# Where a forget bias is added: matrix products against a table, or rows sent through DRAM and added on VectorE

## The chip, the cores and the metric

One core of a Trainium2 chip runs the whole program. The core has TensorE (PE, matrix products and transposes; its weight loads are shown as PEld), VectorE (DVE), ScalarE (ACT), GpSimd (POOL), and SyncE (SP), which issues most of the DMAs. The metric is the device time of one launch in microseconds, lower is better. All data are float32.

## The reference, cut to what matters

The program is one inference step of a hybrid decoder layer for a prompt of 256 tokens and for 8 samples of 8 new tokens each. After one input projection there are a recurrent branch and an attention branch with 16 heads of 64; their merge goes through an output projection, and a mixture of experts (32 experts, 4 of them for each token) follows. The part that the change touches is the attention of the samples, whose keys and values come from 2 cached pages of 128 rows and from the 8 new tokens:

```
lf_all = concat([cache_logf[page_table].reshape(db, past, N_HEADS), logf], axis=1)   # past = 256
ft = swapaxes(cumsum(lf_all, axis=1), 1, 2)
sc = einsum('bqhd,bkhd->bhqk', q, k_all) * scale
bias = ft[:, :, past:, None] - ft[:, :, None, :]
p = softmax(where(mask, sc + bias, -inf), axis=-1)
```

The term of the query is the same for all keys of a row, and a softmax doesn't see it. Both kernels leave it out and add only minus the running sum: one row of 264 numbers for each sample and head, 128 rows in all.

## The kernel before, in words

The instruction streams are written out by hand, one for each engine. Each engine runs its own list in order, and semaphores join them. The pools of memory are few: `ring` (12 units of 2 x 128 x 2048) holds weights, cached keys and values, and, in units 4 and 5 (`fr`), small tables; PSUM has 8 banks, `B[0]` to `B[7]`.

The stages are: conditioning and input projection (to about 195 us), attention of the prompt beside the gate projections (`gate_job`, to about 284 us), attention of the samples beside the last gate jobs and the output projection (to about 378 us), norms and routing (to about 414 us), and then the experts, which read 400 MB of weights through the ring.

What counts here:

- **The cached log-forget pages.** SP loads 16 pages (8 samples, 2 pages, each 128 rows x 16 heads) into `lfc`. In head pair 6 of the prompt's attention, TensorE runs `cached_logf`: 16 products of a 32-column block against the identity, and 4 more for the new tokens, which lay the rows of sample b in the partitions 32 (b mod 4) to 32 (b mod 4) + 15, with the samples 4 to 7 beside the samples 0 to 3. Half of the partitions stay unused.
- **The running sums.** After the last head pair, VectorE copies these rows to `Fs` (L1168 to L1173), scans them in two halves (L1175) and changes the sign (L1176). The semaphore `F_made` reaches 2.
- **The scores of a sample.** `sscores(b)` makes 8 products of queries and keys into `B[2]` (L1733; each is recorded as two instructions, as all float32 products are), and then adds the bias by two more products, of the selection table `hsel` with the rows in `Fs`: 256 columns for the past (L1735), 8 columns for the new tokens (L1736). In `B[2]` the 128 partitions are the 16 heads by the 8 queries.
- **The softmax of a sample.** On VectorE `sample_max(b)` copies the 256 columns from PSUM to `Ss` (L1116), adds the mask to the other 64 (L1117) and takes the maximum (L1120). ScalarE takes the exponential, `sample_norm(b)` scales on VectorE (L1124, L1125), and TensorE turns the result (`sweights`), multiplies it with the values (`svalues`) and folds the heads (`sfold`).
- **The order on TensorE around it.** Gate job `gb` 2, `values(7)`, `sscores(0)`, gate job `gb` 3, `sscores(1)`, `sweights(0)`, and then for b = 0 to 7: a gate job (b < 4) or a quarter of the output projection, `svalues(b)`, `sscores(b+2)`, `sfold(b)`, `sweights(b+1)`. `sscores(b)` waits until `sample_max(b-1)` has read `B[2]` (semaphore `sscores_read`).
- **The order on SP around it.** `values_in(1)`, `chunk(23)`, `chunk(25)` (half of `w_out`, issued when gate job `ga` 7 is done), `keys_in(2)` (8 DMAs of 128 KB), `keys_in(3)`, `chunk(24)`, `keys_in(4)`, and then values and keys in turn. The keys go to two buffers and are turned by VectorE (`keys_turned`, L1108).
- **The join with the experts.** SP issues the first weights of the experts as the last samples free ring units; the ring holds a bit less than one pair of experts, and SP then waits until TensorE has used a unit.

## Time and profile before

| | us |
|---|---|
| median of 3 runs | 1372.84 (1371.81 to 1375.29) |
| the profiled execution, its own time | 1371.63 |
| its span, first to last instruction | 1369.9 |
| TensorE busy | 1302.4 (95%) |
| VectorE busy | 356.7 (26%) |
| ScalarE busy | 207.6 (15%) |
| mean granted TensorE clock | 0.989 |

TensorE is busy nearly throughout, but in the stage of the experts its busy time covers short waits for weights: matrix products are pipelined, and a product that waits inside counts as busy. The chain of waits names both, TensorE and the DMAs of the experts' weights. VectorE, ScalarE and GpSimd have idle time in every stage, which costs nothing unless TensorE or SP waits for them.

### The profile page before, as it was taken

How to read it: one execution, taken by the hardware profiler on the slowest of the kernel's cores; microseconds unless marked ns; L12 is line 12 of the kernel's file. 1: busy time of each engine (PE TensorE's matmuls, PEld its weight loads, DVE VectorE, ACT ScalarE, POOL GpSimd, SP SyncE). 2: the span in 40 equal slices, each digit the busy share in tenths (PEclk: the TensorE clock that was granted, in tenths of full speed). 3: DMA queues.
4: the chain of work that ended last, by engine and by line, in shares of the span. 5: the costliest groups of instructions: out<-in, count | busy, mean ns of one | idle time of the engine just before them, and what ended most of it. 6: DMA issues, size and time to landing. Idle time of an engine off the chain costs nothing.

```text
span 1369.9 us, 15525 instructions
## 1 busy us (share of the span) xinstructions
PE 1302.4 (95%) x6186; PEld 578.7 (42%) x6186; DVE 356.7 (26%) x754; ACT 207.6 (15%) x475; POOL 38.4 (3%) x79
## 2 busy tenths in 40 slices
PE   5999999999999999999999999999999999999896
PEld 3556466655463433434334343333434343343332
DVE  2541325756462121112112111221211121121112
ACT  1124424412221110101001010110101011010101
POOL 1100002000020000000000000000000000000000
PEclk9999999999999999999999999999999999999998
DMA  9836476779676999999999999999999999999992
GB/s 343 281 136 278 185 268 178 217 226 263 222 292 250 416 429 428 427 427 426 427 427 428 428 428 428 427 428 422 428 424 428 428 425 428 422 428 427 428 428 109
DMA packets 71904, 491.06 MB, mean 358 GB/s; under 512 B 11813, under 2 KB 24861, under 8 KB 44052
## 3 DMA queue, kind: packets, MB, share of 16 engines
q1 hardware_dynamic: 68564, 480.86, 86.8%
q0 software_dynamic: 3264, 9.13, 2.5%
q8 instruction: 55, 0.90, 0.3%
q14 instruction: 21, 0.17, 0.0%
HBM read 484.77 MB, written 5.18 MB: 358 GB/s over the span
## 4 chain that ended last, share of the span: by engine, by line
PE 58%; DMA 36%; DVE 2%; issue 1%; SPq 1%; ACT 0%; DVEq 0%; ACTq 0%
DMA ring<-in_w_gate_up_dram 34%; PE bank L1944 23%; PE bank L1627 8%; PE bank L1653 4%; PE bank L1932 2%; PE bank L2002 2%; PE bank L1615 2%; PE bank L1782 2%; PE bank L1567 2%; PE bank L1501 2%; PE bank L2030 1%; PE bank L1935 1%; PE bank L1908 1%; PE bank L1757 1%; DMA ring<-in_cache_k_dram 1%
## 5 line engine op out<-in xcount | busy, mean ns | idle before, releaser
L1944 PE MATMUL bank<-ring,work 128*64 128x512 f32 x1984 | 441.9, 599 | 15.3 <-DMA ring<-in_w_gate_up_dram 9.4
L1944 PEld LDWEIGHTS bank<-ring,work 128*64 128x64 f32 x1984 | 156.4, 138 | 286.7 <-issue 286.7
L1944 PE MATMUL bank<-ring,hT 128*64 128x512 f32 x896 | 201.3, 596 | 11.8 <-DMA ring<-in_w_gate_up_dram 11.6
L1444 DVE TENSOR_TENSOR gbT<-gbT,bank 128x512 f32<-128x512 f32 x80 | 55.0, 688 | 439.2 <-PE bank L1935 304.1
L1944 PEld LDWEIGHTS bank<-ring,hT 128*64 128x64 f32 x896 | 67.8, 137 | 142.5 <-issue 142.5
L1627 PE MATMUL bank<-hT,ring 128*128 128x320 f32 x384 | 106.3, 436 | 1.6 <-DVE hT L910 1.6
L1400 DVE TENSOR_SCALAR work<-bank 128x512 f32<-128x512 f32 x32 | 22.0, 686 | 315.9 <-PE bank L1944 295.4
L1627 PEld LDWEIGHTS bank<-hT,ring 128*128 128x128 f32 x384 | 71.8, 190 | 36.8 <-issue 4.0
L1653 PE MATMUL bank<-hT,ring 128*128 128x320 f32 x256 | 73.6, 437 | 0.2 <-ACT gaT L700 0.2
L1932 PE MATMUL bank<-work 128*128 128x512 f32 x128 | 67.8, 631 | 0.0
L837 ACT ACTIVATE work<-bank 128x320 f32<-128x320 f32 x15 | 6.6, 437 | 395.9 <-PE bank L1501 395.9
L1908 PE MATMUL bank<-qT,tok 128*128 128x256 f32 x224 | 63.3, 405 | 0.0
L1653 PEld LDWEIGHTS bank<-hT,ring 128*128 128x128 f32 x256 | 46.9, 190 | 19.7 <-issue 2.0
L1501 PE MATMUL bank<-ident,work 128*128 128x128 f32 (+4 forms) x250 | 44.5, 297 | 8.8 <-DMA work<-in_b_ada_dram 4.0
L1908 PEld LDWEIGHTS bank<-qT,tok 128*128 128x128 f32 x224 | 37.9, 189 | 28.2 <-issue 25.3
L850 ACT ACTIVATE work<-bank 128x512 f32<-128x512 f32 x30 | 16.3, 594 | 205.7 <-PE bank L1944 205.7
L1501 PEld LDWEIGHTS bank<-ident,work 128*128 128x128 f32 (+4 forms) x250 | 30.6, 175 | 34.8 <-issue 26.2
L840 ACT ACTIVATE work<-work 128x512 f32<-128x512 f32 x30 | 18.9, 630 | 144.6 <-DVE work L1400 144.6
L1932 PEld LDWEIGHTS bank<-work 128*128 128x128 f32 x128 | 20.4, 188 | 46.6 <-issue 46.6
L1909 PE MATMUL bank<-qT,tok 64*128 64x256 f32 x112 | 39.0, 428 | 0.0
L1567 PE MATMUL bank<-ring 128*32 128x512 f32 x192 | 26.3, 675 | 10.2 <-DMA ring<-in_w_ada_dram 10.2
L2002 PE MATMUL bank<-ring,hT 128*64 128x512 f32 x128 | 29.0, 597 | 0.0
(375 smaller groups left out, 911.4 us busy)
## 6 DMA issues: line engine op xcount, KB each, us to landing
ring<-in_w_gate_up_dram SPq DMA_DIRECT2D x128, 2048.0 KB, 16.2
ring<-in_w_down_dram SPq DMA_DIRECT2D x64, 2048.0 KB, 17.3
ring<-in_w_ada_dram SPq DMA_DIRECT2D x12, 2048.0 KB, 10.7
ring<-in_w_in_dram SPq DMA_DIRECT2D x12, 2048.0 KB, 10.8
ring<-in_cache_k_dram SPq DMA_DIRECT2D x64, 128.0 KB, 5.9
ring<-in_cache_v_dram SPq DMA_DIRECT2D x16, 512.0 KB, 5.7
ring<-in_w_out_dram SPq DMA_DIRECT2D x2, 2048.0 KB, 12.2
out_dram<-tok POOLq DMA_DIRECT2D x2, 1024.0 KB, 8.1
```

Of the source, the lines that this page charges most:

```text
L1444: TTo(piece(gbf, i), piece(gbf, i), B[6 + n % 2][:, :], ALU.add).then_inc(s["scatter_read"], 1)
L1501: return nc.tensor.transpose(out, in_, ident[0:rows, 0:rows])
L1567: last = mm(B[3][32 * g:32 * g + 32, :], silu_c[:, 2 * n + k, :], w_[:, k, 512 * g:512 * g + 512], start=(part == 0 and n == 0 and k == 0) ...
L1615: last = mm(ps[:, :], hT[:, k, 128 * n:128 * n + 128], w[0][:, k, :], start=(k == 0), stop=(k == NT - 1))
L1627: last = mm(ps[:, 0:T], w[0][:, k, 128 * (t % 4):128 * (t % 4) + 128], hT[:, k, :], start=(k == 0), stop=(k == NT - 1))
L1653: last = mm(gate_bank(i)[:, 0:T], wg[kind][:, k, 128 * (t % 4):128 * (t % 4) + 128], hT[:, k, :], start=(k == 0), stop=(k == NT - 1))
L1782: last = mm(B[5 + h][:, :], gaT[:, k, 128 * t:128 * t + 128], wo[h][:, k, :], start=(k == 0), stop=(k == NT - 1))
L1908: mm(out, tok[:, k, 128 * m:128 * m + 128], sel[:, k, :], start=(k == 0), stop=False)
L1909: last = mm(out, tok[q:q + 64, 2, 128 * (m % 4):128 * (m % 4) + 128], sel[q:q + 64, 2, :], start=False, stop=True)
L1932: last = mm(bank[:, :], C[:, 128 * k:128 * k + 128], Ysb[:, 512 * (i % 2):512 * (i % 2) + 512], start=True, stop=True)
L1944: last = mm(bank[CAP * x:CAP * x + CAP, :], lhsT[:, CAP * x:CAP * x + CAP], rhs(x), start=start, stop=stop)
L2002: last = mm(B[x + 2 * q][CAP * h:CAP * h + CAP, :], slots[:, k, CAP * x:CAP * x + CAP], gu_slot[4 * x + k // 2][:, k % 2, 1024 * q + 512 * ...
```

## The change

- The pages are laid out in `lfc` so that one 128-column block holds page i of all 8 samples. `cached_logf` becomes two 128x128 transposes and one small product for the new tokens (`lfnew` by `at_token`). Every partition then holds one sample and head: partition 16 b + h.
- The new tokens' values are spread into `lfnew` by one VectorE instruction; two small tables (`in_sample`, `at_token`) are made at the start. The table `hsel` and its four copies go.
- The sign is changed by the copy out of PSUM, and one scan does all rows. This work moves on VectorE ahead of `keys_turned(0)` and the last outputs of the prompt.
- SP writes the 128 rows to DRAM (`sample_bias`, `sample_tail`: 16 DMAs of 16 rows each), waits until they have landed, and reads them back so that each row lies in the 8 partitions of its head's queries: 8 DMAs of 128 KB to the place of the prompt's queries in `qT`, and one of 32 KB (`Ftail`).
- `sscores` loses its two bias products. `sample_max` adds the bias with the copy out of PSUM (`tensor_tensor` instead of `tensor_copy`), and adds the tail to the 8 new columns with one more instruction. `sample_max(0)` waits for the DMAs.

```diff
@@ sync
             chunk(25)
             keys_in(2)
+            eng.wait_ge(s["F_made"], 2)
+            for b in range(DB):
+                rows = Fs[H * b:H * b + H, :]
+                eng.dma_start(sbias_d[b].rearrange("u g n -> g u n"), rows[:, 0:PAST]).then_inc(s["bias_out"], 16)
+                eng.dma_start(stail_d[:, :, b, :].rearrange("u g q -> g u q"), rows[:, PAST:PAST + DS]).then_inc(s["bias_out"], 16)
+            eng.wait_ge(s["bias_out"], 16 + 32 * DB)
+            eng.wait_ge(s["scores_ps"], H)
+            for b in range(DB):
+                eng.dma_start(qT[:, b, 0:PAST], sbias_d[b].rearrange("u g n -> (u g) n").unsqueeze(1).to_broadcast([H, DS, PAST])).then_inc(s["bias_in"], 16)
+            eng.dma_start(Ftail, stail_d.rearrange("u g b q -> (u g) (b q)").unsqueeze(1).to_broadcast([H, DS, NS])).then_inc(s["bias_in"], 16)
             keys_in(3)
             chunk(24)
@@ vector, sample_max
-                V_.tensor_copy(P[:, 0:PAST], ps[:, 0:PAST]).then_inc(s["sscores_read"], 1)
+                if b == 0:
+                    eng.wait_ge(s["bias_in"], 96 + 16 + 16 * DB)
+                TTo(P[:, 0:PAST], ps[:, 0:PAST], qT[:, b, 0:PAST], ALU.add).then_inc(s["sscores_read"], 1)
...
+                new = P[:, PAST + DS * b:PAST + DS * b + DS]
+                link(TTo(new, new, Ftail[:, DS * b:DS * b + DS], ALU.add))
@@ tensor, cached_logf
+                eng.wait_ge(s["sample_consts"], 1)
+                for i in range(NPG):
+                    tr(B[1][:, 128 * i:128 * i + 128], lfc[:, DB * i:DB * i + DB, :].rearrange("p b h -> p (b h)"), 128)
+                mm(B[0][:, 0:DS], lfnew, at_token, start=True, stop=True).then_inc(s["tr_ps"], 1)
@@ tensor, sscores
-                        mm(ps[32 * g:32 * g + 32, 0:PAST + NS], Qbd[:, b % 2, t, :], KT[:, b % 2, t, :],
-                           start=(odd == 0), stop=False)
-                mm(ps[:, 0:PAST], hsel[q:q + H, :], Fs[q:q + H, n, 0:PAST], start=False, stop=False)
-                mm(ps[:, PAST + DS * b:PAST + DS * b + DS], hsel[q:q + H, :], Fs[q:q + H, n, PAST:PAST + DS], start=False, stop=True)\
-                    .then_inc(s["sscores_ps"], 1)
```

SP between `keys_in(2)` and `keys_in(3)` before: the last of the 8 DMAs of one is followed by the first of the next (TENSOR_LOAD and ISA read the page's number).

```order
L431 DMA ring<-in_cache_k_dram 32x4x256
L336 TENSOR_LOAD tiny [waits KT_made]
L336 ISA x2
L431 ISA
L431 DMA ring<-in_cache_k_dram 32x4x256
```

And with the change, the start and the end of what stands there now:

```order
L433 DMA ring<-in_cache_k_dram 32x4x256
L457 DMA sample_bias<-ring 4x4x256 [waits F_made]
L458 DMA sample_tail<-ring 4x4x8
...
L462 DMA qT<-sample_bias 128x1x256 [waits scores_ps,bias_out]
L462 DMA qT<-sample_bias 128x1x256 x7
L463 DMA ring<-sample_tail 128x1x64
L338 TENSOR_LOAD tiny [waits KT_made]
```

25 DMAs and two waits stand between the two loads of keys; `keys_in(3)` and all that SP issues after it come behind them.

VectorE before, from the last output of the prompt to the maximum of sample 0 (L1086 is `head_out`, L1187 makes `fold8`):

```order
L1187 TENSOR_REDUCE work<-ident 128x32 [waits chain_dve]
L1102 COPY work<-qT 32x8x8 x4
L1086 COPY gbT<-bank 128x256 [waits py_ps]
L1116 COPY work<-bank 128x256 [waits sscores_ps]
L1117 TENSOR_TENSOR work<-bank,ring 128x64
L1120 TENSOR_REDUCE tiny<-work 128x1 [waits sscores_read]
```

And with the change, to the turning of the keys of sample 2 (L1159 and L1160 are `gate_tile`, L1141 and L1142 `sample_norm`, L1121 `keys_turned`):

```order
L1199 TENSOR_REDUCE work<-ident 128x32 [waits chain_dve]
L1115 COPY work<-qT 32x8x8 x4
L1099 COPY gbT<-bank 128x256 [waits py_ps]
L1131 TENSOR_TENSOR work<-bank,qT 128x256 [waits bias_in,sscores_ps]
L1132 TENSOR_TENSOR work<-bank,ring 128x64
L1136 TENSOR_TENSOR work<-work,ring 128x8 [waits sscores_read]
L1137 TENSOR_REDUCE tiny<-work 128x1 [waits chain_dve]
L1159 SCALAR_TENSOR_TENSOR gbT<-ring,gbT 128x256 [waits py_read,job_ev]
L1160 SCALAR_TENSOR_TENSOR gaT<-gaT,gbT 128x256 [waits chain_dve]
L1141 RECIPROCAL tiny<-tiny 128x1 [waits sexp_done]
L1142 TENSOR_SCALAR work<-work,tiny 128x320 [waits chain_dve]
L1121 STREAM_TRANSPOSE work<-ring 128x8x8x32 [waits sscores_ps,k_in0]
```

The wait on `bias_in` is new and stands ahead of everything that VectorE does for the samples; the addition of 8 columns is new in each sample.

## Rows read from the trace of the kernel before

**Rows 1.** The page: the chain that ended last, shares by engine.

```profile
PE 58%; DMA 36%; DVE 2%; issue 1%; SPq 1%; ACT 0%; DVEq 0%; ACTq 0%
```

**Rows 2.** Stretches: us, busy us of each engine (instructions), TensorE clock, DMA share, GB/s.

```profile
310.00:320.00 10.00, 10.00 (x85) 6.21 (x84) 6.82 (x18) 1.80 (x6) 0.00 (x0) 1.00 1.11 267
...
410.00:420.00 10.00, 7.71 (x41) 3.02 (x39) 6.98 (x19) 3.35 (x5) 0.00 (x0) 1.00 0.01 2
```

**Rows 3.** TensorE in order of time (start, us, what, [idle before]), `cached_logf`.

```profile
269.49 1.06 PE L1700 MATMUL bank<-ident,ring 128*32 128x128 f32 x8
...
274.36 2.42 PE L1653 MATMUL bank<-hT,ring 128*128 128x320 f32 x8
```

**Rows 4.** The same view, TensorE around the first samples.

```profile
290.22 1.28 PE L1733 MATMUL bank<-work 128*32 128x320 f32 x16 [1.63 <-DVE work L1102]
...
296.69 1.28 PE L1733 MATMUL bank<-work 128*32 128x320 f32 x16
297.90 0.69 PE L1735 MATMUL bank<-ring,vecT 16*128 16x256 f32 x2
298.44 0.28 PE L1736 MATMUL bank<-ring,vecT 16*128 16x8 f32 x2
298.65 0.55 PE L1501 MATMUL bank<-ident,work 128*128 128x128 f32 x3
299.03 4.47 PE L1653 MATMUL bank<-hT,ring 128*128 128x320 f32 x16
```

**Rows 5.** VectorE in order of time, around the first samples.

```profile
289.64 0.38 DVE L1187 TENSOR_REDUCE work<-ident 128x32 f32<-128x128 f32 x1 [0.15 <-DVE gaT L1092]
...
292.29 0.42 DVE L1116 COPY work<-bank 128x256 f32<-128x256 f32 x1 [1.07 <-PE bank L1736]
292.75 0.23 DVE L1117 TENSOR_TENSOR work<-bank,ring 128x64 f32<-128x64 f32 x1
...
294.41 0.39 DVE L1125 TENSOR_SCALAR work<-work,tiny 128x320 f32<-128x320 f32 x1
299.06 2.31 DVE L1108 STREAM_TRANSPOSE work<-ring 128x2048 f32<-128x2048 f32 x1 [4.27 <-DMA ring<-in_cache_k_dram]
...
316.17 0.42 DVE L1116 COPY work<-bank 128x256 f32<-128x256 f32 x1 [1.50 <-PE bank L1736]
```

**Rows 6.** SP's issues in order of time (start, us of issuing): loads of `w_out`, keys.

```profile
282.73 0.39 SPq L370 DMA_DIRECT2D ring<-in_w_out_dram  x1
283.87 5.80 SPq L431 DMA_DIRECT2D ring<-in_cache_k_dram  x8
```

**Rows 7.** The same view: small loads, and reads of `bias_rows`.

```profile
5.34 0.29 SPq L381 DMA_DIRECT2D work<-in_g_ffn_pre_dram  x1
5.67 0.29 SPq L381 DMA_DIRECT2D work<-in_g_ffn_post_dram  x1
...
245.37 0.36 SPq L390 DMA_DIRECT2D work<-bias_rows  x1
245.77 0.51 SPq L391 DMA_DIRECT2D work<-bias_rows  x1
```

**Rows 8.** DMA issues (xcount, KB, median us to landing): 170 to 192 us.

```profile
ring<-in_w_in_dram SPq DMA_DIRECT2D x1, 2048.0 KB, 15.3
...
bias_rows<-ring SPq DMA_DIRECT2D x1, 16.0 KB, 15.1
```

**Rows 9.** The same view: 245.3 to 245.6 us, and 251 to 258 us.

```profile
work<-bias_rows SPq DMA_DIRECT2D x1, 256.0 KB, 3.9
...
ring<-in_cache_k_dram SPq DMA_DIRECT2D x9, 128.0 KB, 4.1
```

**Rows 10.** TensorE in order of time: after an idle stretch, and the same work later.

```profile
14.68 3.64 PE L1567 MATMUL bank<-ring 128*32 128x512 f32 x16 [10.20 <-DMA ring<-in_w_ada_dram]
...
22.99 1.92 PE L1567 MATMUL bank<-ring 128*32 128x512 f32 x16
```

**Rows 11.** Stretches as in rows 2: the end of the program, TensorE idle.

```profile
1362.00:1363.00 1.00, 0.00 (x0) 0.00 (x0) 1.00 (x2) 0.32 (x2) 0.00 (x0) 0.50 0.03 8
```

More of the change, by code:

```diff
@@ L110, in hybrid_layer @@
         rs = fr[:, 3368:3688]
-        lfcf, lftf = fr[:, 2432:2432 + 272], fr[:, 4008:4096]
+        in_sample, at_token = fr[0:NS, 4056:4056 + DB], fr[0:NS, 4064:4064 + DS]
+        lfnew = fr[0:NS, 2688:2816]
         lfz = fr[0:H, 3688:4008]
@@ L215, in hybrid_layer @@
         Fp = rs[0:H, 0:SP_]
[L216 removed]
+        Fs = fr[:, 0:PAST + DS]
+        Ftail = fr[:, PAST + DS:PAST + DS + NS]
         def few(a, n, parts=128):
@@ L1018, in _ @@
             STT(lfz, acc_, -2.0, lfz, ALU.mult, ALU.add).then_inc(s["lf_made"], 1)
-            for g in range(4):
-                q = 32 * g
-                V_.tensor_copy(hsel[q:q + H, :].rearrange("k (u g c) -> k u g c", u=4, c=DS),
-                               ident[q:q + H, q:q + H].rearrange("k (g u) -> k u g", u=4).unsqueeze(3).to_broadcast([H, 4, 4, DS]))\
-                    .then_inc(s["hsel_made"], 1)
-            eng.wait_ge(s["consts_made"], 5)
+            eng.wait_ge(s["consts_made"], 4)
             eng.wait_ge(s["lf_made"], 1)
@@ L1151, in _ @@
                 if p == NT - 1:
+                    eng.wait_ge(s["tr_ps"], G_CF + 1)
+                    link.later(TS(Fs[:, 0:PAST], B[1][:, 0:PAST], -1.0, None, ALU.mult))
+                    link(TS(Fs[:, PAST:PAST + DS], B[0][:, 0:DS], -1.0, None, ALU.mult))
+                    link(V_.tensor_copy(r1, ones[:, 0:2]))
+                    V_.tensor_tensor_scan(Fs, onesf, Fs, 0.0, ALU.mult, ALU.add).then_inc(s["F_made"], 1)
                     eng.wait_ge(s["scores_read"], H)
@@ L1166, in _ @@
                     head_max(2 * p + 5)
-            eng.wait_ge(s["tr_ps"], G_CF + 1)
-            link.later(V_.tensor_copy(Fs[:, :, 0:PAST], B[1][:, :].rearrange("p (s c) -> p s c", s=2)))
-            for g in range(4):
-                q = 32 * g
-                ins = V_.tensor_copy(Fs[q:q + 32, :, PAST:PAST + DS], B[0][q:q + 32, 0:NS].rearrange("p (s c) -> p s c", s=2)[:, :, DS * g:DS * g + DS])
-                link.later(ins)
-            link(V_.tensor_copy(r1, ones[:, 0:2]))
-            for n in range(2):
-                link(V_.tensor_tensor_scan(Fs[:, n, :], onesf, Fs[:, n, :], 0.0, ALU.mult, ALU.add))
-            TS(Fs, Fs, -1.0, None, ALU.mult).then_inc(s["F_made"], 1)
             queries(0)
```

37 lines of the change are left out of this document (17 added, 20 removed).

## The prediction, made before the changed kernel ran

> **What bounds the kernel now.** I read first the page's chain: it is TensorE for 58% and DMA for 36% of the span [rows 1]. The DMA part is the stage of the experts, whose weights must pass at what the DMA engines give. Then I looked for the moment when that stage starts, in the table of stretches: from 410 to 420 us the DMA engines move 2 GB/s [rows 2]. The ring is full there and SP waits for TensorE to use the first units. So both streams of the experts' stage, the products and the weights, start from one event on TensorE at about 414 us. Whatever reaches that point earlier or later moves the end by the same amount, and nothing in the change touches the experts. What leads up to it is TensorE again: 10.00 us busy of 10.00 between 310 and 320 us [rows 2]. The question is therefore how much TensorE's list between 269 and 365 us becomes shorter, and whether a new wait enters it.
>
> I work in the times of the profile of before, and ask how much earlier or later each step stands.
>
> **The cached pages.** `cached_logf` takes from 269.49 to 274.36, that is 4.87 us, on a busy TensorE [rows 3]. In its place come two transposes of 128x128 and one small product. Three products of the transposing kind take 0.38 us (298.65 to 299.03) [rows 4], so I take 0.45 us for the new three. **Gain 4.4 us.** VectorE's scan moves ahead of the turning of keys 0, which costs VectorE about 1.5 us at a place where it is idle until TensorE delivers. It also leaves VectorE's list ahead of `fold8` at 289.64 [rows 5], for which TensorE waited 1.63 us at 290.22 [rows 4] (the row names L1102, a neighbour). The copies, two scans and the sign there are about 4 us, more than that wait. TensorE would come at 284.2 and find `fold8` done by about 282. **Gain 1.6 us.**
>
> **The bias products.** One sample's two bias products take from 297.90 to 298.65, 0.75 us [rows 4]. Eight of them: **gain 6.0 us**, if TensorE stays busy around them. VectorE pays for them with one more small instruction in each sample: the addition with the copy costs about what the copy cost, 0.42 us, and the 8 columns, with their wait for the one before, about 0.25 us (L1117 with 64 columns takes 0.23 [rows 5]). In the steady samples VectorE sits idle 1.50 us until the scores come [rows 5], so this is hidden.
>
> Up to here 12.0 us would be gained: 4.4 + 1.6 + 6.0. Edits that I cost at nothing: the two small tables at the start and `lfnew` (VectorE waits for others there), and the four copies of `hsel` and one memset that go.
>
> **The way through DRAM.** TensorE now arrives at `sscores(1)` at 296.69 - 4.4 - 1.6 - 0.75 = **289.9** [rows 4]. `sscores(1)` needs `B[2]` read by `sample_max(0)`, and that now waits for the rows from DRAM. When do they land? Step by step:
>
> 1. SP issues the load of `w_out` when gate job `ga` 7 is done, at 282.73, and the 8 DMAs of keys until 289.67 [rows 6]. Both shift by 4.4: SP is free for the writes at 285.3. `F_made` came at about 273 and isn't waited for.
> 2. Sixteen writes of 16 rows. Small loads are issued 0.33 us apart (5.34, 5.67) [rows 7]: 5.4 us, to 290.7.
> 3. Their landing. A 16 KB write behind a load of 2 MB landed when that load did: 15.1 and 15.3 us, issued 0.4 us apart [rows 8]. So these writes stand behind `w_out` and the keys, which landed at 299.06 when VectorE turned them [rows 5], and come at 294.7 now. For sixteen of them I add 1.3 us: 296.0.
> 4. Nine reads, 0.40 us (245.37 to 245.77) [rows 7] to 0.5 us apart: the last of 128 KB is issued at about 299.6. A read of `bias_rows` landed after 3.9 us with little in its way, keys of 128 KB after 4.1 us [rows 9]: **303.7**. The bounds: with issues at the short end, writes that land with the keys, and no addition, 300.5; if a read behind seven others takes as long as keys do where the engines are full, about 308.
>
> The Trainium skill (page "DMA: Bandwidth & Descriptors", section "Anatomy of one DMA — SWDGE (gpsimd) path") gives a DMA a fixed cost of about 2.0 us and bytes / 436e3; that read would then land at about 302 instead of 303.7, and the sum below would be +2.9 us, called an estimate. No row here shows a lone 128 KB read, so the 3.9 us stay.
>
> **The wait and what is behind it.** Before, `sample_max(0)` began at 292.29, its result was scaled by 294.80, and the gate job that follows `sweights(0)` began at 299.03 [rows 4, 5]. Now: the begin at 303.7, 2.75 us to the scaled result with the new addition, 0.1 us, and 0.4 us for `sweights(0)`: that gate job begins at 306.9, **7.9 us later** than before. From there on six samples (2 to 7) save 0.75 us each, 4.5 us. Sum: 7.9 - 4.5 = **+3.4 us**. All gains ahead of the wait are swallowed by it, since TensorE only waits longer: about 14 us, from 289.9 to 304.5.
>
> Queued behind the wait on VectorE stand `gate_tile(2)`, `sample_norm(0)` and the turning of keys 2. Those keys are turned by 309, `sscores(2)` comes at about 313: no second wait. On SP `keys_in(3)` stands behind the nine reads, is issued from 300 to 305 and lands before 311, and VectorE wants it at 316; `chunk(24)` is wanted at 336. Both have room.
>
> **The clock.** An idle TensorE loses its clock: the granted share reads 0.50 at the end of the program, two us after its last product [rows 11]. After the idle stretch of 10.20 us at the start the same sixteen instructions took 3.64 us, and 1.92 us later in the program [rows 10]. That is half the clock, 1.2 instead of 2.4 GHz, for the first 3.6 us or so, 1.7 us lost. Here part of it falls into the wait for the scaled result (0.85 us), so I take **+1.2 us**, between 0 and 2.5.
>
> **The sum.** +3.4 + 1.2 = +4.6 us on the profiled execution: 1371.63 becomes 1376.2. Against the median of the runs, 1372.84, it is **1377.4 us**. The range of this case alone is +1.5 to +8.
>
> **The rivals.**
>
> *The round trip is quick and the clock holds.* Landing at 300.5 gives 3.4 - 3.2 = +0.2 us, with a clock cost of 0 to 1.2: about 1373.5. For it: by the short ends of steps 2 to 4 nothing forbids it. Against it: it needs all of them.
>
> *The writes are slow in the queues.* SP's writes are views of 4 x 4 rows, and the few rows of one may not be spread over all 16 DMA engines. Rows of 1 KB, as the keys are, move at about 267 GB/s over 16 engines [rows 2], that is 61 ns a row on one engine. If all sixteen writes go over 4 engines, each has 64 pieces behind the keys, 3.9 us if a short piece costs as much, instead of 1.3: landing at 306.3, and the sum is +7.2, or 1380. The Trainium skill (page "DMA: Bandwidth & Descriptors", section "Why a DMA increments its semaphore by 16 and not by 1") says that the number of engines must divide the slowest dimension of both sides, which would be 4 here; no row of this trace shows how such a DMA is spread.
>
> *The loop doesn't become shorter.* The DMA share between 310 and 320 us is 1.11 [rows 2]. If keys and values set the pace of the samples, the 4.5 us of the later samples aren't gained: +9.1 us, 1382. Against it: TensorE doesn't wait once for keys there, and about 2.1 MB a sample at that rate are 7.9 us of the 8.1 that are left. That is close, and the reads have put more in front.
>
> *It is faster.* Decided by one point: when `sample_max(0)` is let go. At or before 289.2 the whole 12 us would be gained; SP's issues alone, to 285.3 + 5.4 + 3.6, exclude that. If the writes overtake the keys in the queues and land at 292.5, and the nine reads follow in 3.6 us, the last landing 1 us behind its issue, the begin is at 297 with a short stall: 3.4 - 6.7 = -3.3 us, and one more us on any of the steps above (the keys earlier because less else is loaded) passes -4.1: about 1368.5.
>
> **How the numbers follow.** A measurement of this kernel tells about 0.3%, 4.1 us, from no change. Forecast 0.52 (two thirds of it above +4.1), slow writes 0.13, loop not shorter 0.10, quick 0.18, faster 0.07. Slower: 0.34 + 0.13 + 0.10 = 0.57. Same: 0.18 + 0.18 = 0.36. Faster 0.07. The range from 1371.5 to 1383 leaves out most of the faster case and what is worse than +10.
>
> **What the profile would show.** `cached_logf` in three instructions and half a us; no wait of TensorE for `fold8`; one wait of TensorE ahead of the second group of score products, put down to VectorE's addition, of some 14 us, and on VectorE a wait of some 19 us for a DMA that writes `qT`; the granted clock at 0.50 around it; then a period of 8.1 instead of 8.9 us for a sample; and the experts starting at about 418.5 instead of 414. The forecast is wrong if the reads land before 300 or after 308, if the period stays at 8.9, or if a second wait stands at the keys of sample 3 or 4.

## The result, and the profile after

The changed kernel takes **1378.34 us** (median; 1373.6 to 1383.44), the kernel before 1373.04 us when timed beside it. The ratio is **1.0039, with a 95% interval from 1.0028 to 1.0050**: about 5.3 us slower. The prediction said 1377.4 us, and on the profiled execution +4.6 us; that of after takes 1376.96 us instead of 1371.63, +5.3 us (span 1375.3 instead of 1369.9).

TensorE of after in order of time (start, us, what, [idle before and what ended it]), from the cached pages to the second period of the loop:

```profile
269.41 0.38 PE L1513 MATMUL bank<-ident,ring 128*128 128x128 f32 x2
269.72 0.38 PE L1710 MATMUL bank<-ring 64*128 64x8 f32 x2
270.04 2.42 PE L1665 MATMUL bank<-hT,ring 128*128 128x320 f32 x8
...
284.21 1.28 PE L1739 MATMUL bank<-work 128*32 128x320 f32 x16
...
305.77 2.36 PE L1739 MATMUL bank<-work 128*32 128x320 f32 x16 [15.78 <-DVE work L1132]
308.06 0.90 PE L1513 MATMUL bank<-ident,work 128*128 128x128 f32 x3
308.76 4.53 PE L1665 MATMUL bank<-hT,ring 128*128 128x320 f32 x16
...
316.96 4.47 PE L1665 MATMUL bank<-hT,ring 128*128 128x320 f32 x16
...
325.10 4.47 PE L1665 MATMUL bank<-hT,ring 128*128 128x320 f32 x16
```

Read beside [rows 3, 4]: the cached pages take 0.63 us instead of 4.87. `sscores(0)` at 284.21 has no wait ahead of it, where there was one of 1.63 us. Then comes a stall of 15.78 us that wasn't there, and the gate job that follows `sweights(0)` begins at 308.76 instead of 299.03, 9.7 us later. From there the period is 8.14 us (316.96 to 325.10) instead of 8.89, which is the distance of these two rows of the kernel before:

```profile
308.13 4.47 PE L1653 MATMUL bank<-hT,ring 128*128 128x320 f32 x16
...
317.02 4.47 PE L1653 MATMUL bank<-hT,ring 128*128 128x320 f32 x16
```

What ended the stall, on VectorE of after. The first row is `sample_max(0)`, the last the first addition of a later sample:

```profile
305.07 0.42 DVE L1131 TENSOR_TENSOR work<-bank,qT 128x256 f32<-128x256 f32 x1 [20.32 <-DMA ring<-sample_tail]
...
307.57 2.30 DVE L1121 STREAM_TRANSPOSE work<-ring 128x2048 f32<-128x2048 f32 x1
...
316.14 0.42 DVE L1131 TENSOR_TENSOR work<-bank,qT 128x256 f32<-128x256 f32 x1 [0.79 <-PE bank L1739]
```

The 20.32 us end with the last of the nine reads. The two new additions cost 0.42 (L1131) and 0.17 us (L1136), and a later sample still finds VectorE 0.79 us early, so they are hidden there.

SyncE's issues of after (start, us of issuing), and under them, from the DMA view, the size and the median us to landing:

```profile
285.64 0.92 SPq L457 DMA_DIRECT2D sample_bias<-ring  x1
...
287.27 0.58 SPq L457 DMA_DIRECT2D sample_bias<-ring  x1
287.90 0.59 SPq L458 DMA_DIRECT2D sample_tail<-ring  x1
...
295.40 0.58 SPq L458 DMA_DIRECT2D sample_tail<-ring  x1
297.78 5.07 SPq L462 DMA_DIRECT2D qT<-sample_bias  x8
302.90 0.60 SPq L463 DMA_DIRECT2D ring<-sample_tail  x1
```

```profile
qT<-sample_bias SPq DMA_DIRECT2D x8, 128.0 KB, 2.5
...
ring<-sample_tail SPq DMA_DIRECT2D x1, 32.0 KB, 2.1
```

The round trip in three pieces: sixteen writes, one every 0.625 us, are issued in 10.3 us (285.64 to 295.98); 1.8 us later they have landed; nine reads are issued in 5.7 us, and the last lands 2.1 us after its issue.

Stretches of after (us; busy us of TensorE, its weight loads, VectorE, ScalarE, GpSimd; TensorE's clock; DMA share; GB/s):

```profile
290.00:296.00 6.00, 0.00 (x0) 0.00 (x0) 0.00 (x0) 0.00 (x0) 0.00 (x0) 0.94 0.80 171
296.00:308.00 12.00, 2.23 (x16) 0.68 (x16) 2.79 (x9) 1.15 (x4) 0.00 (x0) 0.50 0.44 135
308.00:310.00 2.00, 2.00 (x12) 1.59 (x9) 2.00 (x2) 0.00 (x0) 0.00 (x0) 0.78 0.68 201
310.00:320.00 10.00, 10.00 (x84) 6.08 (x83) 8.13 (x27) 2.99 (x10) 0.00 (x0) 1.00 1.05 305
```

TensorE does nothing from 290 on, and the granted clock falls to 0.50, the lower of its two levels (1.2 instead of 2.4 GHz). It rises again between 308 and 310, with TensorE at work since 305.77. The DMA share of 0.44 between 296 and 308 is the other thing to notice: the DMA engines, which also carry keys and values, are more than half idle there, where the kernel before has a share of 1.08 to 1.13 from 295 to 310.

### The profile page after: what moved, and what is told of

Read it like the earlier page. It is cut to its first block, busy times and chain, and to the rows that moved or that the text cites. A ratio compares the mean times of both kernels' runs of the same rounds, so it can differ in the third digit from the quotient of the medians.

```text
span 1375.3 us, 15416 instructions
## 1 busy us (share of the span) xinstructions
PE 1292.2 (94%) x6118; PEld 571.8 (42%) x6118; DVE 357.4 (26%) x756; ACT 207.5 (15%) x475; POOL 38.1 (3%) x78
## 4 chain that ended last, share of the span: by engine, by line
PE 54%; DMA 40%; SPq 2%; DVE 2%; issue 1%; ACT 0%; DVEq 0%; ACTq 0%
DMA ring<-in_w_gate_up_dram 37%; PE bank L1946 21%; PE bank L1639 8%; PE bank L1665 4%; PE bank L2004 2%; PE bank L1627 2%; PE bank L1786 2%; PE bank L1934 2%; PE bank L1513 2%; PE bank L1579 1%; DMA ring<-in_w_in_dram 1%; PE bank L2032 1%; PE bank L1937 1%; PE bank L1761 1%; SPq L498 1%
```

## The experiments

Every profile of a kernel starts this stage at a slightly different time (the first transposes of `cached_logf` between 266.48 and 271.71), so places are compared by their distance from that instruction. **D** below is the distance from there to the first product of `out_proj(0)`; up to there stand the scores of the first six samples and the values of the first four. In the kernel before it is 65.3 us (269.49 [rows 3] to 334.80), in after 72.0 (269.41 to 341.39), 6.7 more. Ratios are to the kernel before on the same chip, with their 95% interval.

| kernel | ratio | interval | D, us |
| --- | --- | --- | --- |
| after | 1.0039 | 1.0028 to 1.0050 | 72.0 |
| turned_only | 0.9998 | 0.9982 to 1.0014 | 69.1 |
| early_25 | 1.0027 | 1.0015 to 1.0039 | 73.4 |
| few_late | 1.0025 | 1.0011 to 1.0039 | 72.3 |
| few_first | 0.9995 | 0.9982 to 1.0008 | 69.1 |
| turned_order | 0.9950 | 0.9931 to 0.9969 | 59.8 |
| before_order | 0.9986 | 0.9967 to 1.0005 | 67.7 |
| turned_plain | 0.9996 | 0.9977 to 1.0015 | 65.7 |
| before_plain | 0.9997 | 0.9979 to 1.0015 | 66.2 |
| no_bias | 0.9949 | 0.9935 to 0.9963 | 61.9 |
| no_bias_order | 0.9930 | 0.9905 to 0.9956 | 59.6 |
| plain_writes | 1.0025 | 1.0002 to 1.0047 | 73.3 |
| trip_pool | 0.9930 | 0.9907 to 0.9952 | 59.1 |

D comes from one profiled execution of each kernel and the ratio from many. They don't always agree: in turned_only and few_first D is 3.8 us longer than in the kernel before and the ratio shows no difference, and before_order's D is 2.4 us longer with a ratio of 0.9986. A D holds whatever of the lower clock fell into that one execution (in before_order it fell on a gate job, 6.26 instead of 4.57 us). So D says where time went in one execution, and verdicts rest on the ratios. They can't tell a difference of less than about 3 us from none. Differences in us to the kernel before are worked out from them.

### One half of the change alone

**turned_only.** The new turning and the one scan; the bias is still added by two products on TensorE, and nothing goes through DRAM.

```diff
-            for b in range(DB):
-                rows = Fs[H * b:H * b + H, :]
-                eng.dma_start(sbias_d[b]..., rows[:, 0:PAST])...
...
+                pick = hsel[q:q + 32, b % 2, :]
+                mm(ps[:, 0:PAST], pick, Fs[q:q + 32, 0:PAST], start=False, stop=False)
+                mm(ps[:, PAST + DS * b:PAST + DS * b + DS], pick, Fs[q:q + 32, PAST:PAST + DS], start=False, stop=True)
```

> Only the new turning of the cached pages, with the one scan and its earlier place; the bias stays two products on TensorE (with a selection table of 32 rows), and nothing goes through DRAM. Theory (the waits for the rows from DRAM swallow real gains): 4.4 us from the turning and 1.6 us from the vanished wait for VectorE show in full, -6.0 us against the kernel before, ratio 0.9956, and the first samples' scores begin at 284.2. Rival (the gains ahead of the samples never were on the path, since keys or VectorE take over as the late ones): within 1 us of the kernel before, and a new wait of TensorE for keys or VectorE near 284 or 298 us.

Measured: 1372.54 us, ratio 0.9998. The 6 us that I had added up for this half are on TensorE's list and not in the time. TensorE of turned_only, and the row of VectorE that it traces back to:

```profile
291.99 4.47 PE L1659 MATMUL bank<-hT,ring 128*128 128x320 f32 x16
300.36 1.93 PE L1759 MATMUL bank<-ring,work 128*32 128x256 f32 x16 [3.90 <-ACT work L769]
```

```profile
295.78 2.31 DVE L1119 STREAM_TRANSPOSE work<-ring 128x2048 f32<-128x2048 f32 x1 [8.01 <-DMA ring<-in_cache_k_dram]
```

The gate job that stood at 299.03 is at 291.99. Behind it TensorE waits 3.90 us for the turned weights of sample 0. ScalarE copies them only after the exponentials of sample 1 (299.09), these wait for `sample_max(1)`, and that stands on VectorE behind the turning of keys 2, which land at 295.8. In the kernel before VectorE waited 4.27 us for the same keys [rows 5], and it cost nothing since TensorE had work until 303.5. What follows the wait runs at half clock, and in this execution that costs more than the wait. Stretches of turned_only:

```profile
300.00:310.00 10.00, 9.64 (x66) 5.16 (x67) 5.50 (x15) 2.08 (x8) 0.00 (x0) 0.50 0.97 246
310.00:315.00 5.00, 5.00 (x14) 3.16 (x12) 2.37 (x9) 0.00 (x0) 0.00 (x0) 0.69 0.92 301
```

Counted from `cached_logf`, the gate job stands 5.9 us earlier than before (23.6 instead of 29.5) and `out_proj(0)` 3.8 us later (D). Between them 9.7 us are lost: 3.7 by the wait, and the other 6.0 while the clock is low. So **a second limit stood close behind TensorE, the arrival of sample 2's keys, and running into it costs the clock as well.** The rival's numbers were met.

The 6.0 us are those of one execution, which took 1375.67 us, 3.1 more than the median of its kernel. Two other kernels of the table meet the same keys. In turned_plain TensorE waits 4.12 us, and from the values of sample 0 to those of sample 1 it needs 11.28 us where 8.89 are usual, 2.4 us lost; in no_bias it waits 5.58 us, and 1.6 us are lost behind it (9.73 instead of 8.14). TensorE of turned_plain:

```profile
299.11 1.94 PE L1758 MATMUL bank<-ring,work 128*32 128x256 f32 x16 [4.12 <-ACT work L768]
...
310.39 1.07 PE L1758 MATMUL bank<-ring,work 128*32 128x256 f32 x16
```

### The round trip made shorter or earlier, with the transfers as they were

**early_25** puts the writes and reads ahead of `chunk(25)` (the second half of `w_out`) and of `keys_in(2)`:

```diff
             chunk(23)
+            (16 writes, wait, 9 reads)
             chunk(25)
             keys_in(2)
-            (16 writes, wait, 9 reads)
```

> The changed kernel with its 16 writes and 9 reads issued ahead of the second half of w_out and the keys of sample 2, as soon as the sums are made at 273.1. Theory (the place in SP's list and the issuing set the moment): writes issued to 283.2, landed by 285, reads issued to 290.7, last landing at 293, 12 us earlier than in the changed kernel. The keys of sample 2 are then issued at 292 behind 2 MB and come late by 2 to 3 us: -4 to -7 us against the kernel before. Rival (contention or slower samples cost the time, not this wait): still +3 us or more.

Measured: 1376.18 us, 1.0027, which isn't told from the changed kernel (the intervals overlap), and at +3.7 us it is the number of the rival. Counted from `cached_logf` the rows land 9.2 us sooner than in after, of the 12 that the theory had, and TensorE's stall for the bias falls by as much, from 15.78 to 6.58 us. But a new one of 8.49 us appears, behind keys 2 that are now issued at 293. VectorE, then TensorE of early_25:

```profile
305.09 2.31 DVE L1121 STREAM_TRANSPOSE work<-ring 128x2048 f32<-128x2048 f32 x1 [9.41 <-DMA ring<-in_cache_k_dram]
```

```profile
309.88 1.93 PE L1761 MATMUL bank<-ring,work 128*32 128x256 f32 x16 [8.49 <-ACT work L777]
```

The two stalls together are 15.07 us, so what was gained at one was lost at the other. The theory had those keys late by 2 to 3 us.

**few_late** leaves the place and halves the writes: 8 of 32 rows, strided over the samples.

```diff
-            for b in range(DB):
-                rows = Fs[H * b:H * b + H, :]
+            for u in range(4):
+                rows = Fs[u:128:4, :]
```

> The changed kernel with 8 writes (32 rows each) in place of 16, same place, 9 reads as they are. If SP's issuing alone sets the landing of the writes: they are issued in 5.0 instead of 10.2 us and everything behind is 5 us earlier, +0.3 us against the kernel before. If the queue of loads ahead (w_out, keys of sample 2, landing at about 294.5) is the next limit: the writes land at about 296 instead of 297.8, 2 us earlier: +3.5 us. If neither (fixed latency of a write to DRAM): no difference from the changed kernel, +5.4 us.

Measured: 1376.49 us, 1.0025, which is +3.4 us with an interval from +1.5 to +5.4: the middle one of the three expected numbers, with the least excluded and the largest not. D doesn't get shorter (72.3): the rows are there 1.1 us sooner, but the gate job behind the stall takes 5.96 us at the lower clock, and 4.53 in after. The writes are issued in half the time, and the wait for their landing grows in return. SyncE of few_late:

```profile
288.20 0.57 SPq L458 DMA_DIRECT2D sample_tail<-ring  x1
294.55 5.08 SPq L462 DMA_DIRECT2D qT<-sample_bias  x8
```

5.8 us from the last write to the first read, where the changed kernel has 1.8. The DMA share stays above 1 until 291.5 and is down at 0 only at 293.5. The same eight writes stand in few_first (below) ahead of `w_out` and the keys, and there the first read goes out 1.6 us after the last write:

```profile
275.89 0.57 SPq L456 DMA_DIRECT2D sample_tail<-ring  x1
278.02 5.41 SPq L460 DMA_DIRECT2D qT<-sample_bias  x8
```

So it is what stands in front that makes the same writes wait 4.2 us longer, as step 3 of the prediction had it. Which of the two, issue or queue, ends last in after was a matter of about 1.4 us (this profile runs 1.9 us ahead, so its 294.55 answers to 296.4 against 297.78).

**few_first** puts 8 writes and the 9 reads first, then keys 2, then `chunk(25)`.

> 8 writes and 9 reads ahead of everything, as soon as the sums are made, then the keys of sample 2, then the second half of w_out. Theory: rows there at about 288.5 us, before TensorE's second group of score products at 289.9, so the whole gain of the two edits shows: -12 us against the kernel before, ratio 0.9913, no wait of TensorE there, no half clock. Rival (a wait takes the place of the one removed: keys of sample 2, or VectorE's longer list per sample): -6 to -9 us with a wait of 3 us or more near 298.

Measured: 1372.44 us, 0.9995: the loss of the change is gone, and no gain came; neither expectation had that. The waits for keys that the rival put near 298 come at 293 and again at 312 to 318. VectorE of few_first:

```profile
290.69 0.42 DVE L1131 TENSOR_TENSOR work<-bank,qT 128x256 f32<-128x256 f32 x1 [7.63 <-DMA ring<-sample_tail]
...
295.31 2.31 DVE L1121 STREAM_TRANSPOSE work<-ring 128x2048 f32<-128x2048 f32 x1 [2.04 <-DMA ring<-in_cache_k_dram]
...
318.54 2.31 DVE L1121 STREAM_TRANSPOSE work<-ring 128x2048 f32<-128x2048 f32 x1 [5.97 <-DMA ring<-in_cache_k_dram]
```

Each wait that is shortened gives its place to one for keys. That is the pattern to be explained: is it the order of the transfers, or are the DMA engines short of time?

### The order of the transfers

**turned_order** is turned_only with three transfers moved.

```diff
             chunk(23)
-            chunk(25)
             keys_in(2)
+            chunk(25)
             keys_in(3)
-            chunk(24)
             keys_in(4)
             for b in range(2, DB):
                 values_in(b)
                 if b + 3 < DB:
                     keys_in(b + 3)
+                if b == 2:
+                    chunk(24)
...
-            eng.dma_start(x1..., x_prompt...)     (GpSimd, at PT_ps, with x_sample)
...
             eng.dma_start(hf[:, 0:2 * D], of_prompt(3, 5))...
+            eng.wait_ge(s["sv_ps"], 5)
+            eng.dma_start(x1..., x_prompt...)
```

> turned_only with its transfers in another order: SyncE issues the keys of sample 2 ahead of the second half of w_out, the first half of w_out only after the keys of sample 5, and GpSimd fetches the residual input again only after svalues(4) instead of at 284. Theory (the 6 us that turned_only frees on TensorE ahead of 292 are given back because the DMA engines are full from 280 on and sample 2's keys land at 295.8 behind w_out): keys_turned(2) waits less than 1 us instead of 8.01, TensorE's wait of 3.90 ahead of svalues(0) and the half clock behind it go, and 6 us are left: ratio to the kernel before 0.9957, 1367 us. Rival (the wait moves on to values or to later keys, the stretch holds too many bytes for any order): within 1.5 us of before, ratio 0.999 to 1.001, with a wait for cache_k, cache_v or w_out of 3 us or more later in the loop.

Measured: **1368.7 us, 0.9950 (0.9931 to 0.9969)**, 6.9 us below the kernel before by the ratio and 5.5 by the medians. TensorE of turned_order:

```profile
292.58 4.47 PE L1661 MATMUL bank<-hT,ring 128*128 128x320 f32 x16
296.98 1.07 PE L1761 MATMUL bank<-ring,work 128*32 128x256 f32 x16
```

No wait and full clock where turned_only had 3.90 us and half clock; the period is 8.89 and D is 5.6 us shorter than in the kernel before. The keys of sample 2 are issued at 275.57, in a stretch that the kernel before leaves unused: there the DMA engines move nothing from 275 to 280, because SyncE waits in front of `chunk(25)` until 282.73 [rows 6] with the keys behind it. Stretches of the kernel before and of turned_order:

```profile
275.00:280.00 5.00, 5.00 (x27) 3.25 (x25) 0.00 (x0) 0.82 (x2) 0.00 (x0) 1.00 0.00 0
...
295.00:300.00 5.00, 5.00 (x34) 3.13 (x33) 0.94 (x1) 0.61 (x2) 0.00 (x0) 1.00 1.13 234
```

```profile
295.00:300.00 5.00, 5.00 (x49) 2.37 (x48) 1.93 (x8) 0.61 (x2) 0.00 (x0) 1.00 0.40 114
```

**before_order** is the control: the same order in the kernel before.

> The kernel before with the same order of transfers as turned_order and nothing else. It says what the order is worth by itself. Both theories: TensorE waits for no transfer between 284 and 345 in the kernel before, so the order frees nothing: 0 +- 1 us, ratio 0.9995 to 1.0007. If it is faster by 3 us or more, the gain of turned_order is the order's and not the new turning's.

Measured: 1372.28 us, 0.9986 (0.9967 to 1.0005). The order alone is within the noise, and the gain of turned_order is in the main that of the new turning, let through. Between the two the ratio differs by 0.0036, some 5 us, and their intervals only just overlap; by these numbers 1.9 of the 6.9 us could be the order's own. Which of the three moved transfers does it wasn't tried apart.

**turned_plain and before_plain** ask whether the form of the keys matters: four transfers a page of 32 whole rows instead of 128 quarter rows.

```diff
-                    rows = cache_k[0, ds(page(eng, NPG * b + i), 1), :, :, :].rearrange("o (m r) h d -> r (o m) (h d)", r=32)
+                    rows = cache_k[0, ds(page(eng, NPG * b + i), 1), :, :, :].rearrange("o p h d -> (o p) (h d)")
                     for g in range(4):
-                        eng.dma_start(kv[32 * g:32 * g + 32, b % 2, i, :].rearrange("p (m n) -> p m n", m=4),
-                                      rows[:, :, 256 * g:256 * g + 256])...
+                        eng.dma_start(kv[32 * g:32 * g + 32, b % 2, i, :], rows[32 * g:32 * g + 32, :])...
```

> turned_only with the keys of each page fetched as four transfers of 32 whole rows (4 KB packets) instead of four of 128 quarter rows (1 KB packets): same bytes, same number of transfers, and the keys then stand in the wrong order, so the sample outputs are not the reference's. Theory (the DMA engines are the second limit, and quarter rows hold them to about 235 GB/s where w_out moves at 390): keys take two thirds of the time, keys_turned(2) waits 2 to 4 us less than its 8.01, later waits go, and 4 to 7 us are left against before_plain: ratio to before 0.995 to 0.997. Rival (it is not the DMA engines' time but the place of the keys behind w_out in the queue, or the half clock): no more than 1.5 us off turned_only, 1371 to 1374.

> The kernel before with the keys fetched in 4 KB packets, as in turned_plain (sample outputs are not the reference's). Both theories: its TensorE does not wait for transfers in the loop, so 0 to -1 us, 1371.5 to 1373; the DMA engines' busy share between 295 and 340 falls from 1.09 to 0.8.

Measured: 0.9996 and 0.9997. My theory of the small packets fell: VectorE of turned_plain still waits 8.2 us for keys, the DMA share of before_plain stays near 1 and doesn't fall to 0.8, and the engines move whole rows no faster. A stretch of before_plain:

```profile
295.00:300.00 5.00, 5.00 (x28) 3.52 (x21) 2.51 (x2) 0.00 (x0) 0.00 (x0) 1.00 1.05 242
```

242 GB/s at a share of 1.05, against 234 at 1.13 with quarter rows. The place of the keys behind 2 MB of `w_out` counts, and not the length of their rows. One thing was the same in both forms and stays untested: each of these transfers goes to 32 of the 128 partitions.

### The floor, and what the round trip costs

**no_bias** is the changed kernel without writes, reads and additions; **no_bias_order** is the same with the order of turned_order.

```diff
-            (16 writes, wait, 9 reads)
...
-                TTo(P[:, 0:PAST], ps[:, 0:PAST], qT[:, b, 0:PAST], ALU.add)...
+                V_.tensor_copy(P[:, 0:PAST], ps[:, 0:PAST])...
-                link(TTo(new, new, Ftail[:, DS * b:DS * b + DS], ALU.add))
```

> The changed kernel without its round trip (bias neither written, read nor added) and with its own order of transfers: the second half of w_out ahead of the keys of sample 2, the residual input fetched at 278. Theory (without the stall for the round trip, the changed kernel would still meet the full DMA engines): a wait of 5 us or more on VectorE for cache_k near 296, and no more than 4 us of the 12 left: ratio 0.997 to 1.000, 1368 to 1373. Rival (the round trip is the only loss): 0.9913, 1361, as no_bias_order.

> The changed kernel without its round trip: the samples' forget bias is scanned but never written, read or added (so the sample outputs leave it out), with the transfers in the order of turned_order. It is the floor of the change. Theory: 12 us below the kernel before, 0.9913, and within 1 us of trip_pool. Rival: 0.995, as turned_order, with the 6 us of the products given back in waits for transfers.

Measured: no_bias 1366.55 us, 0.9949; no_bias_order 1362.8 us, 0.9930 (0.9905 to 0.9956), between its theory of 0.9913 and its rival of 0.995 and told from neither. For no_bias both numbers that I had written down were off: the ratio lies between theory and rival. It meets the keys, as the theory said. VectorE and TensorE of no_bias:

```profile
299.30 2.31 DVE L1111 STREAM_TRANSPOSE work<-ring 128x2048 f32<-128x2048 f32 x1 [8.93 <-DMA ring<-in_cache_k_dram]
```

```profile
303.88 1.93 PE L1747 MATMUL bank<-ring,work 128*32 128x256 f32 x16 [5.58 <-ACT work L767]
```

VectorE's wait for them is 8.93 us, TensorE's 5.58, and what that left of the 12 was 7. So the round trip, as the change makes it, costs 1.0039 - 0.9949 = 0.0090, some 12 us, against a kernel that has none (the two were timed on different chips, each against the kernel before).

**plain_writes** asks why a write is issued every 0.625 us: the rows keep their order (16 rows to 16 rows).

```diff
-                eng.dma_start(sbias_d[b].rearrange("u g n -> g u n"), rows[:, 0:PAST])...
+                eng.dma_start(sbias_d[b].rearrange("u g n -> (u g) n"), rows[:, 0:PAST])...
```

> The changed kernel, whose 16 writes keep the order of the rows (16 rows of 256 columns to 16 rows, two-dimensional on both sides, instead of 4 x 4 rows turned), so that the heads get each other's bias and the sample outputs are not the reference's. Theory (0.58 us is what a write from SBUF costs SyncE whatever its shape): still one every 0.62 us, and the chain as in the changed kernel, 1378. Rival (the turned 4 x 4 rows cost it): one every 0.33 us, the last write issued 4.7 us earlier, and 1373.5 to 1375.

Measured: 1377.29 us, 1.0025 (1.0002 to 1.0047). SyncE of plain_writes:

```profile
292.48 0.42 SPq L457 DMA_DIRECT2D sample_bias<-ring  x1
292.94 0.42 SPq L458 DMA_DIRECT2D sample_tail<-ring  x1
297.35 5.06 SPq L462 DMA_DIRECT2D qT<-sample_bias  x8
```

Neither side had it: 0.42 us each and one every 0.46 us, between 0.33 and 0.625. The turned 4 x 4 rows cost 0.16 us a write. All sixteen take 8.6 us instead of 10.3, where the rival wanted 5.3, and the wait from the last of them to the first read is 4.0 us instead of 1.8 (TensorE's stall is 16.48 us). Here the queue in front explains only a part: the DMA share is down at 0 at 294.8, 2.5 us before the first read, where in after and few_late that takes 1.0 us. What the landing waited for in those 2.5 us no view shows.

### A version that hides the round trip

**trip_pool** is the changed kernel with its round trip taken apart: four strided writes of the 256 columns on SyncE ahead of `keys_in(2)`, the tails and all reads on GpSimd's queue, whose engine is idle there, the two reads that `sample_max(0)` needs first and with a semaphore of their own, and the transfers in the order of turned_order.

```diff
             chunk(23)
+            eng.wait_ge(s["F_made"], 2)
+            for u in range(4):
+                eng.dma_start(sbias_d[:, u, :, :], Fs[u:128:4, 0:PAST]).then_inc(s["bias_out"], 16)
             keys_in(2)
             chunk(25)
...
+            (GpSimd) 4 writes of stail_d, wait, read of Ftail, bias_back(0)
             eng.wait_ge(s["PT_ps"], H)
             eng.tensor_copy(KT[:, 1, :, PAST:PAST + NS], kT[:, :, SP_:T]).then_inc(s["tailk_made"], 1)
+            for b in range(1, DB):
+                bias_back(b)
```

> The changed kernel with its round trip hidden: four writes of the 256 columns on SyncE ahead of keys_in(2), four writes of the tails and all nine reads on GpSimd's queue, the first two reads with a semaphore of their own, and the transfers in the order of turned_order. Theory (both parts of the change free TensorE, 6 us by the turning and 8 x 0.75 us by the bias products, where neither the round trip nor the keys are waited for): VectorE's wait for the bias is under 2 us, the period is 8.14 us instead of 8.89, and the ratio to the kernel before is 0.9913, 1361 us. Rival (what the bias products leave is given back, since the stretch is then short of bytes or GpSimd's reads come late): 0.995 to 0.997, no better than turned_order, with a wait for a transfer of 3 us or more in the loop.

Measured: **1364.99 us, 0.9930 (0.9907 to 0.9952)**, 9.6 us below the kernel before by the ratio (8.8 by the medians) and the same as no_bias_order: the round trip costs nothing that can be measured any more, with some 3 us to either side in both numbers. The ratio lies between the theory (0.9913) and the rival (0.995). VectorE of trip_pool at `sample_max(0)` and `sample_max(1)`:

```profile
285.52 0.42 DVE L1143 TENSOR_TENSOR work<-bank,qT 128x256 f32<-128x256 f32 x1 [0.81 <-PE bank L1751]
...
291.39 0.42 DVE L1143 TENSOR_TENSOR work<-bank,qT 128x256 f32<-128x256 f32 x1 [1.06 <-DMA qT<-sample_bias]
```

That the second half of the change, the bias products, pays here isn't shown. Against turned_order, which keeps those products, the ratio is lower by 0.0020, 2.7 us where six were expected, and the intervals overlap; D is 59.1 against 59.8, where six pairs of products are 4.5 us. TensorE of trip_pool says where they are in this execution:

```profile
323.13 1.58 PE L1773 MATMUL bank<-ring,work 128*32 128x256 f32 x16 [2.74 <-issue]
```

The period is 8.14 until 315.92 (307.78 to 315.92), then 2.74 us are lost at the values of sample 3 and about 1.7 more at the lower clock behind them (1.58 instead of 1.07 us, and so on), while the DMA share is 1.12. The row puts the wait down to nothing that the profile shows. `svalues` waits for its values' two transfers, which SyncE issues from 309.47 on, right behind `chunk(24)` at 308.28; the second goes out at about 310.5 and lands 12.5 us later, at about 323.0, and TensorE goes on at 323.13. So the transfer is very likely what it waits for, and much of the rival's case holds: a wait for a transfer, 2.7 us where it had 3 or more. no_bias_order has the same wait (3.3 us) at the same place, so it isn't the round trip; turned_order, 8.89 us a sample, waits only 0.52 us there. Whether `chunk(24)` two samples earlier would take it away wasn't tried.

## Why the prediction came out

**The place of the end.** The argument that what reaches the experts' stage later ends later by as much holds. `out_proj(0)` is 6.6 us later, the router's first product 5.1 (379.35 to 384.45), and the second expert products stand at 424.23 instead of 419.47, 4.8 us later; the end is 5.3 later.

**The cached pages** (forecast -4.4): 4.87 - 0.63 = 4.2 us. **The wait for `fold8`** (-1.6): gone. **The bias products** (8 x 0.75): the period falls by 0.75, and after the stall 9.7 - 5.1 = 4.6 us come back for the forecast 4.5. All of what was gained ahead of the wait was swallowed by it, as forecast: TensorE arrives at 289.99 (forecast 289.9) and stands still for 15.78 us (forecast 14.6 by its own times).

**The round trip, step by step.**

| step | forecast | measured |
| --- | --- | --- |
| 1. SyncE free for the writes | 285.3 | 285.64 |
| 2. sixteen writes issued | 0.33 apart, until 290.7 | 0.625 apart, until 295.98 |
| 3. landed | 296.0 | 297.78 |
| 4. eight reads issued; last landing | 299.6; 303.7 | 302.85; 305.07 |
| next gate job | 306.9, 7.9 later | 308.76, 9.7 later |

Step 2 is the term that was mis-sized: I took the issue of a plain small load for that of a write of 4 x 4 turned rows, and 0.30 us a write, 4.8 in all, was missing. It did little harm, 1.4 us or so, since the queue in front held the writes almost as long (step 3, which few_late beside few_first confirms: its writes were issued by 290.6 in the time of after and read at 296.4, nearly the forecast's 290.7 and 296.0). Step 4 held two errors of opposite sign: an issue every 0.63 us instead of 0.40 to 0.5 made the nine reads 2 us longer, and the landing took 2.1 us, not 3.9 to 4.1. Of the rows these were taken from [rows 9], the 3.9 us belong to 256 KB at a DMA share of 0.47, and the 4.1 to keys at 1.1. The reads of this round trip found the engines half empty (share 0.44); few_first's, with `w_out` and keys not yet issued but GpSimd's 1.3 MB under way, took 6.6 us.

The Trainium skill (page "DMA: Bandwidth & Descriptors", section "Anatomy of one DMA — SWDGE (gpsimd) path") would have been nearer here: it fits a fixed 2.0 us and the bytes' time for DMAs of GpSimd's queue, which for 128 KB is about 2.3 us by estimate. SyncE's reads of 128 KB took 2.5 us in this trace and the one of 32 KB 2.1, so the trace agrees in after, and not in few_first.

**The clock** (forecast +1.2, 0 to 2.5): at the lower level the second group of scores took 2.36 instead of 1.28 us, and the transposes 0.90 instead of 0.55, of which 0.85 fell into a wait anyway; from VectorE's begin to the gate job it is 3.7 us against the 3.2 that I had without the clock, so 0.5.

**The sum, and the luck in it.** Up to the router the terms are 9.7 - 4.6 = +5.1 us for the forecast 7.9 + 1.2 - 4.5 = +4.6. The round trip let TensorE go 1.3 us later than forecast and the clock took 0.7 less, so two errors cancel in part, and so do the two inside step 4. The mechanism is the one forecast; that the total came within 1 us is partly luck.

A second effect of the clock wasn't foreseen. The experts' first sixteen products run at half clock in after and not in before. Of after, then of before:

```profile
417.03 5.35 PE L1946 MATMUL bank<-ring,work 128*64 128x512 f32 x16 [0.21 <-issue]
...
424.23 3.65 PE L1946 MATMUL bank<-ring,work 128*64 128x512 f32 x16
```

```profile
413.97 3.65 PE L1944 MATMUL bank<-ring,work 128*64 128x512 f32 x16 [0.33 <-issue]
```

It is no loss by itself. The kernel before has its dip some 20 us earlier, in the gathering products (1.63 us for four that otherwise take 1.13, 2.62 for six that take 1.54). That is why the experts start at 417.03, not at the forecast 418.5, and are yet 4.8 us late one unit on.

**The rivals.** *Quick round trip*: out, landing at 305.07. Its bound of 300.5 doesn't follow from its own terms: writes landed at 294.7, seven intervals of 0.40 and 3.9 us make 301.4, and +1.1 instead of +0.2 us. (`F_made` "at about 273" is no reading of the kernel before, whose sign change ends at 285.0; in after the scan ends at 273.1.) *Slow writes*: with the turned rows the first read goes out at 297.78, and with sixteen plain rows at 298.5 in the time of after, although their last write was issued 1.5 us sooner. So the turned shape isn't seen to land later. The Trainium skill (page "DMA: Bandwidth & Descriptors", section "Why a DMA increments its semaphore by 16 and not by 1") has the number of engines divide the slowest dimension of both sides, 4 here and 16 in plain_writes. No view shows the spread, and the better one by that rule didn't land sooner. *The loop not shorter* (1382): the period is 8.14, so it was wrong for this kernel, but the reason given for it, the share of 1.11, was sound. The stall let keys and values get ahead, and with them the loop ran at 8.14 without a wait. Where the stall is taken away or shortened and the keys of sample 2 still stand behind other work, a wait appears (turned_only, early_25, few_first, no_bias). *Faster*: I excluded it for this order of issues, rightly; trip_pool shows that a kernel with both parts of the change can be 0.7% faster than the kernel before, of which turned_order has 0.5%.

**What was wrong without showing in the number**: the sentence that 12.0 us would be gained but for the round trip. With the kernel's own order of transfers it is 7.0 (no_bias), and for the turning alone nothing (turned_only). I had looked at VectorE's wait of 4.27 us for the keys of sample 2 [rows 5], used it to date the landing, and didn't ask what it becomes when all in front of it moves 6 us up. It is a wait that costs nothing with TensorE as the bound and takes its place as soon as TensorE is relieved.

## What to carry to other kernels

A wait that costs nothing on an engine beside the bound marks the next limit: before adding up what the bound would gain, subtract its slack, and look on which queue, and behind what, the transfer that ends it stands. Here three moved transfers turned a gain of nothing into one of 6.9 us by the ratio. A round trip through DRAM costs its issues on the queue first of all (25 of them, 16 us here), so issue it when its data is ready, on a queue whose engine is idle, with the piece that is needed first in front.

## What the runs showed of the hardware

- A DMA costs its queue's engine a time that depends on its shape: 0.29 us for a plain row load [rows 7], 0.42 for 16 plain rows, 0.58 for 4 x 4 turned rows, 0.63 for a read spread over 16 x 8 partitions, on SyncE.
- A 128 KB read lands 2.5 us after its issue with the engines half empty. Keys of the same size, issued right behind 2 MB of `w_out`, landed 11.3 us after theirs (after, from 279.55), and 5.3 us in the loop of the kernel before at a share of 1.11 (both are medians). Eight writes of up to 32 KB had landed 1.6 us after the last issue with the engines nearly idle (few_first) and 5.8 us after it behind `w_out` and keys (few_late).
- Rows of 4 KB moved no faster than rows of 1 KB into the same place (242 and 234 GB/s at full share), while the stretches in which 2 MB of `w_out` move show about 400 (394 from 285 to 290 in the kernel before). What makes the difference wasn't settled.
- A stall of 15.8 us costs TensorE's clock for about three us of work behind it, 0.5 us in all in after, since most of the lower level fell into the stall. A stall of about 4 us can be the dearer one: 6.0 us in turned_only, where the lower level came as TensorE began to work again and stayed from 300 to past 310, and 2.4 us in turned_plain after the same wait. So the price of a short stall isn't fixed, and each of these is one execution. This I had not expected at all: I had priced the clock with the stall, not against it.
